# The expert number of a search is formed on GpSimd instead of VectorE, between two gathers

## What is computed

```python
s1, i1 = lax.top_k(s[:, :, 0], PEER_TOPK)            # 16 best of 128 keys, twice
s2, i2 = lax.top_k(s[:, :, 1], PEER_TOPK)
cand_s = (s1[..., :, None] + s2[..., None, :]).reshape(T, PEER_HEADS, PEER_TOPK * PEER_TOPK)
cand_e = (i1[..., :, None] * PEER_KEYS + i2[..., None, :]).reshape(T, PEER_HEADS, PEER_TOPK * PEER_TOPK)
top_s, sel = lax.top_k(cand_s, PEER_TOPK)
eid = jnp.take_along_axis(cand_e, sel, axis=-1)      # the expert numbers
gate = jax.nn.softmax(top_s, axis=-1)
act = jax.nn.gelu(jnp.einsum('thkd,td->thk', u_tab[eid], xt).astype(jnp.float32), approximate=False)
w = (gate * act).astype(xt.dtype)
return jnp.einsum('thk,thkd->td', w, v_tab[eid])
```

## Time and profile before

| | |
|---|---|
| median of 3 runs | 3986.89 us (3982.22 to 3993.07) |
| the profiled execution | 3986.96 us, its span 3984.8 us |
| VectorE busy | 2691.8 us, 68% |
| GpSimd busy | 1225.4 us, 31%, 1024 gathers and 64 casts |
| TensorE busy | 3115.6 us, 78% |
| moved by the DMA engines | 1295.14 MB, of it 1073.81 MB by gathers |

### The profile page before, as it was taken

The page is one execution under the profiler, slowest core; times in us unless marked ns, Lnnn a source line. Parts: engine busy times, 40 slices in busy tenths (PEclk is TensorE's granted clock), DMA queues, the critical chain, the costliest instruction groups (busy, mean ns, idle before and its releaser), DMA issues. The chain is left out here.

```text
span 3984.8 us, 31095 instructions
## 1 busy us (share of the span) xinstructions
PE 3115.6 (78%) x7816; PEld 1412.6 (35%) x7816; DVE 2691.8 (68%) x5254; ACT 1377.4 (35%) x3574; POOL 1225.4 (31%) x1092
## 2 busy tenths in 40 slices
PE   8979999897889989878777877888765656556656
PEld 4545555543434434433333332333322222222222
DVE  3345545312477767777778777868888887888884
ACT  3213333202344344334333423343333334334332
POOL 0000000000233324433344343434444444444442
PEclk9988898798999999989889998889888878878887
DMA  4330101255899999999999999999999999999996
GB/s 160 118 141 24 44 29 37 97 209 222 349 393 414 393 360 421 418 418 378 417 398 417 361 393 391 426 355 411 424 412 399 424 419 389 420 414 393 426 422 265
DMA packets 212916, 1295.14 MB, mean 325 GB/s; under 512 B 24608, under 2 KB 38176, under 8 KB 69408
## 3 DMA queue, kind: packets, MB, share of 16 engines
q0 software_dynamic: 147456, 1073.81, 65.5%
q1 hardware_dynamic: 59552, 207.15, 13.8%
q10 hardware_dynamic: 5760, 12.59, 0.8%
HBM read 1253.60 MB, written 39.85 MB: 325 GB/s over the span
## 5 line engine op out<-in xcount | busy, mean ns | idle before, releaser
L1297 PE MATMUL l_acc<-l_rows,l_diag 128*128 128x512 f32 x2560 | 1422.6, 698 | 732.0 <-ACT l_diag L1431 718.4
L1198 POOL DMA_INDIRECT l_rows<-in_peer_uv,l_at x1024 | 1189.6, 1162 | 1732.1 <-DVE l_acc L1577 1082.3
L1567 DVE SCALAR_TENSOR_TENSOR l_rows<-l_rows,l_xn 128x1024 f32<-128x1024 f32 x1024 | 1227.1, 1224 | 320.2 <-DMA l_rows<-in_peer_uv,l_at 259.8
L1297 PEld LDWEIGHTS l_acc<-l_rows,l_diag 128*128 128x128 f32 x2560 | 526.2, 218 | 1563.6 <-ACT l_diag L1431 1025.8
L1577 DVE SCALAR_TENSOR_TENSOR l_acc<-l_rows,l_wts,l_acc 128x1024 f32<-128x1024 f32 x384 | 492.6, 1283 | 135.0 <-ACT l_wts L1427 135.0
L1423 ACT ACTIVATE l_dots<-l_dots 128x2 f32<-128x2 f32 x512 | 103.8, 203 | 1080.8 <-DVE l_rows L1567 1076.0
L1191 POOL CAST l_at<-l_expert 128x16 uint32<-128x16 f32 x64 | 35.7, 557 | 978.8 <-DVE l_expert L1553 978.5
L117 PE MATMUL l_pa<-all_ring,l_xt 128*128 128x512 f32 x656 | 296.9, 604 | 17.6 <-DMA l_xt<-kept_xnt 17.2
L117 PE MATMUL l_pa<-l_ring,l_xt 128*128 128x512 f32 x624 | 285.1, 608 | 18.2 <-DMA l_xt<-kept_xnt 12.3
L1427 ACT ACTIVATE l_wts<-l_dots,l_gates 128x1 f32<-128x1 f32 x1024 | 293.5, 287 | 16.8
L1431 ACT ACTIVATE l_diag<-all_ident,l_wts 128x128 f32<-128x128 f32 x640 | 257.1, 402 | 21.0
(11 more groups left out here) (241 smaller groups left out, 2780.4 us busy)
## 6 DMA issues: line engine op xcount, KB each, us to landing
l_ring<-in_w_late SPq DMA_DIRECT2D x44, 1024.0 KB
all_ring<-in_w_late SPq DMA_DIRECT2D x44, 1024.0 KB
l_rows<-in_peer_uv,l_at POOLq DMA_INDIRECT x1024
l_yt<-kept_yt SPq DMA_DIRECT2D x48, 256.0 KB, 12.4
kept_s<-l_yt ACTq DMA_DIRECT2D x32, 256.0 KB
l_s_in<-kept_s SPq DMA_DIRECT2D x64, 128.0 KB
mix_w_branches<-in_w_branches_kept SPq DMA_DIRECT2D x8, 768.0 KB, 4.5
kept_yt<-b_yt SPq DMA_DIRECT2D x8, 768.0 KB
```

The costliest lines, as they stand in the source:

```text
L1198: pool.indirect_dma_start(out=rows[:, r % SLOTS, :], out_offset=None, in_=A["peer_uv"], in_offset=bass.IndirectOffsetOnAxis(ap=at[:, c % 2 ...
L1297: ins = pe.matmul(acc2[:, hs], diag[n_pe(r) % DIAGS][:], rows[:, r % SLOTS, D + half * HB:D + (half + 1) * HB], start=first, stop=last)
L1567: dve.scalar_tensor_tensor(out=u, in0=u, scalar=1.0, in1=xn[:, t % 2, :], op0=ALU.mult, op1=ALU.mult, accum_out=dots[:, n:n + 1]).then_inc ...
```

## The change

VectorE keeps only the comparison of `choose`. Product and sum go to GpSimd: one product of 512 elements to a partition, then five additions that each halve the 32 lanes of a winner (256, 128, 64, 32 and 16 elements), then the cast of lane 0, strided, into `at`. GpSimd does this for head c+1 between the 12th and the 13th gather of head c, and for head 0 ahead of the first gather. `hot` isn't doubled, so VectorE's next `search_pairs` waits until the cast is done, and ScalarE's next `convert` waits until the product has read `top_f`.

```diff
+CHOSEN_AT = 12
...
         @block.gpsimd
         def _(pool):
+            hots = [P, TOPK, 2, TOPK]
+
+            def choose(q):
+
+                pool.wait_ge(marked, q + 1)
+                pool.tensor_tensor(hot[:], hot[:], top_f[:].unsqueeze(1).to_broadcast(hots), ALU.mult).then_inc(picked, 1)
+                pool.wait_ge(picked, q + 1)
+                width = 2 * TOPK
+                lanes = hot[:].rearrange("p a k b -> p a (k b)")
+                for n in range(5):
+                    width //= 2
+                    pool.tensor_tensor(lanes[:, :, 0:width], lanes[:, :, 0:width], lanes[:, :, width:2 * width], ALU.add).then_inc(added, 1)
+                    pool.wait_ge(added, q * 5 + n + 1)
+                pool.tensor_copy(at[:, q % 2, :], lanes[:, :, 0]).then_inc(at_ready, 1)
+
             def row(r):
 
                 c, n = divmod(r, TOPK)
+                if c == 0 and n == 0:
+                    choose(0)
+                if n == CHOSEN_AT and c + 1 < PH * T:
+                    choose(c + 1)
                 if n == 0:
-                    pool.wait_ge(chosen, c + 1)
-                    pool.tensor_copy(at[:, c % 2, :], expert[:, c % 3, :]).then_inc(at_ready, 1)
                     pool.wait_ge(at_ready, c + 1)
...
             def convert(q):
 
                 act.wait_ge(parts_ready, q + 1)
+                wait(act, picked, q)
...
             def search_pairs(q):
+                wait(dve, at_ready, q)
...
             def choose(q):
                 dve.wait_ge(converted, q + 1)
-                wait(dve, at_ready, q - 2)
-                order(tt(hot[:], part_f[:].rearrange("p k a -> p a k").unsqueeze(3).to_broadcast(hots),
-                         R["iota16"][:].unsqueeze(1).unsqueeze(1).to_broadcast(hots), ALU.is_equal))
-                order(tt(hot[:], hot[:], top_f[:].unsqueeze(1).to_broadcast(hots), ALU.mult))
-                ins = dve.tensor_reduce(expert[:, q % 3, :], hot[:].rearrange("p a k b -> p a (k b)"), AX.X, ALU.add)
-                ins.then_inc(chosen, 1)
-                dve.wait_ge(chosen, q + 1)
+                tt(hot[:], part_f[:].rearrange("p k a -> p a k").unsqueeze(3).to_broadcast(hots),
+                   R["iota16"][:].unsqueeze(1).unsqueeze(1).to_broadcast(hots), ALU.is_equal).then_inc(marked, 1)
                 dve.wait_ge(exp_ready, q + 1)
```

More of the change, by code:

```diff
@@ L994, in late_stage @@
         soft, total = sb("soft", [P, 2, TOPK]), sb("total", [P, 2, 3])
-        expert, gates = sb("expert", [P, 3, TOPK]), sb("gates", [P, 3, TOPK])
+        gates = sb("gates", [P, 3, TOPK])
         at = sb("at", [P, 2, TOPK], U32)
@@ L1030, in late_stage @@
         (merged_done, rms_done, rms_ready, xs_ready, prms_done, prms_ready, prstd_ready, out_ready, dve_step, act_step,
-         searched, best_ready, parts_ready, converted, neg_ready, exp_ready, sum_ready, gate_ready, chosen, at_ready,
+         searched, best_ready, parts_ready, converted, neg_ready, exp_ready, sum_ready, gate_ready, marked, picked, added, at_ready,
          dot_done, act_done, wts_ready, diag_ready, acc_done, acc2_done, h2_ready, h2t_ready) = (sem(n) for n in (
              "merged_done rms_done rms_ready xs_ready prms_done prms_ready prstd_ready out_ready dve_step act_step "
-             "searched best_ready parts_ready converted neg_ready exp_ready sum_ready gate_ready chosen at_ready "
+             "searched best_ready parts_ready converted neg_ready exp_ready sum_ready gate_ready marked picked added at_ready "
              "dot_done act_done wts_ready diag_ready acc_done acc2_done h2_ready h2t_ready").split())
```

## The result

The changed kernel takes 4060.22 us (median of 4 runs, 4054.83 to 4069.88) against 3986.95: a ratio of 1.0195, 95% interval 1.0175 to 1.0216 (the quotient of the two medians is 1.0184). It is 73 us slower. I had said 4070.

A forecast was written before the change was run, and what follows sets the result against it. No engine was full; DMA transfers limited the second stretch, gathers from 2700 to 3900 us. Late queue 64 + 36, prologue 3, less 17 for VectorE's freed time: +86 us on 3986.96, so 4073, said as 4070; range 3960 to 4180.

The forecast's parts named there:

- The allowance: Between the 12th and 13th gathers: GpSimd may start the next gather 4.1 us late before the DMA engines run dry.
- The block's length: GpSimd's seven instructions ahead of the 13th gather: 3.5 + 1.2 + 1.6 = 6.3 us, between 3.0 and 12.1.
- The price of a late queue: Gathers behind the block: queue dry 2.2 us a head; 64 us for 29 saturated heads, 36 for 33 earlier ones.
- The credit for VectorE's freed time: VectorE loses 1.44 us a head: nothing directly in the saturated stretch, 17 us gained in the first.
- faster: Rival, chance 0.17: slots limit, not the queue; VectorE's freed time brings slots free sooner, around 3950 us.
- New waits: Candidate sum and ScalarE's conversion don't wait for the block; the first gather in the prologue comes 3 us later.
- GpSimd gives way, VectorE doesn't: Rule weighed for SBUF reads: casts wait for dots, dots never lengthen; a product would hold VectorE by the skill's rule.
- Where the waits for rows show: Sign in VectorE's dots: waits up from 3.5 us a head, the largest on the row issued behind the block.
- DMA share: Sign in the stretch from 2700 to 3900 us: share down from 1.00 to about 0.95.
- heavy: Rival, chance 0.12: each GpSimd instruction waits for a whole VectorE instruction; block 12.1 us, about 4350 us.
- my case: Main forecast, chance 0.50: late gathers slow the kernel to between 4010 us (block 4.8 us) and 4180 (block 9 us).

The follow-up runs named there:

- three pauses: The kernel before with 20, 32 or 42 dependent 16-element GpSimd memsets ahead of each head's 13th gather, VectorE's work kept: 1.0033, 1.0143 and 1.0278.
- the run with 32 memsets: The kernel before with 32 dependent 16-element GpSimd memsets ahead of each head's 13th gather, VectorE's work kept: 4035.7 us, ratio 1.0143.

## Why the prediction was right, step by step

- **The allowance (4.1 us).** Right, as far as three pauses can tell: 3.9 us of pause cost 0.33%, 6.0 us 1.43%. They place the bend near 4 us and not to a tenth, and the 13 us for a pause inside the allowance were not in my sum. It came from four gathers in flight, 2.45 us a row and 6.4 us for a gather into an empty queue.
- **The block's length (6.3 us).** Right, 6.1 us in the head shown, and in part by luck. GpSimd's instructions by shape in the first block, with nothing beside them:

```profile
L1192 POOL TENSOR_TENSOR l_hot<-l_hot,l_top_f 128x512 f32<-128x512 f32 x1 | 1.3, 1262 | 973.9 <-DVE l_hot L1569 973.9
L1198 POOL TENSOR_TENSOR l_hot<-l_hot 128x256 f32<-128x256 f32 x1 | 0.7, 726 | 0.1
```

  The slope is (1262 - 726) ns over 256 elements, 2.09 ns, twice VectorE's as I had put it, and the seven take 3.4 us for my 3.5. But the six gaps come to 0.45 us where I had 1.2, and the waits against VectorE in the head shown to 2.05 us where I had 1.6 (5.91 us from the product's start to the cast's end, for 3.86 in the first block). The two errors offset each other for the most part.
- **The price of a late queue.** Right in direction, too high in size. I charged 2.2 us a head in the second stretch and half of that in the first, 64 + 36 us. By GB/s the whole loss is 48 + 27, and the pause of the block's length costs only 1.43%, some 56 us. The error is that I let each microsecond beyond the allowance cost a whole one in the second stretch and a half in the first. The pauses show 0.7 to 0.8 in the second stretch, and 0.33 to 0.5 over all heads.
- **The credit for VectorE's freed time (17 us).** Wrong: worth nothing (1.0007). This also settles the *faster* rival: less work on VectorE brings no slot free soon enough to matter. That the number came so close, 86 predicted for 73, is partly luck: the queue was charged 100 us where a pause of that length costs 56, the credit was 17 us too high, and the 16 to 20 us (0.4 to 0.5%) that the changed kernel loses on top of such a pause stood nowhere in the sum.
- **New waits.** Right. VectorE's candidate sum and ScalarE's conversion don't wait for GpSimd: neither stands in the view of waits with GpSimd as the one waited for. The first gather starts 4.15 us after the product's start where it was 1.95: 2.2 us, I had 3.
- **GpSimd gives way, VectorE doesn't.** I left open what a product would do. It holds VectorE: 2802 ns for a dot. The Trainium skill (SBUF — State Buffer, "Who interferes with whom") says that a VectorE instruction with two SBUF inputs and a GpSimd instruction that reads SBUF exclude each other. The trace now agrees on both sides: the dot of 2802 ns, and a cast of 16 elements that takes 1.07 us at 3533.76 beside a dot. The holding also spoils a number of mine: VectorE's busy time fell by 33 us and not by 88, because 55 us of holding are counted in it.
- **Where the waits for rows show.** I expected the largest at the row behind the block. They come three rows later and in the next head. The 13th row has several microseconds between landing and its dot: by the landings in the trace, 3.8 us in the mean of heads 34 to 62, for 4.0 before, because its transfer, issued late, takes 5.1 us from the issue's end for 8.8 before.
- **DMA share.** I expected 0.95 and it is 0.98; the rate tells it better, 397 for 413 GB/s.
- The *heavy* rival's mechanism exists (the block ahead of the 9th gather, 9.25 us in one head), but not in the place that the change chose.
- The bounds of my case don't follow from their own terms: 3987 + 223 - 14 is 4196, where I wrote 4180, and a block of 4.8 us gives 4005 for 4010. The measured time lies far from both.

**What is left.** The changed kernel's 1.0195 stands 0.4 to 0.5% above the pauses of its length (1.0143 and 1.0152, the interval of the second overlaps with it). The rates say it too, in both stretches: 389 and 397 GB/s, for 391 and 400 in the run with 32 memsets and 391 and 399 in the run without product and sum and with 30 memsets. The granted clock doesn't explain it, 0.887 in the changed kernel's profiled execution and 0.888 in that last run's. That reads cost something just where the queue is thin would fit: the held weighing frees a slot later. No run isolates it, so it stays open. No placement made the kernel faster than before. The run without product and sum (1.0007, 0.9994 to 1.0019) leaves none to gain more than 0.06% by VectorE's freed time.

## What to carry to other kernels

Here the engine that issues the transfers had an allowance between two issues: what is in flight, times the time of one transfer, less the latency into an empty queue, 4.1 us. Work put there was almost free up to it (0.33%). Beyond it, each microsecond cost 0.7 to 0.8 us where the transfers run back to back, and 0.33 to 0.5 us over the whole kernel. Work out the same three numbers for your kernel. Cut the work up and put the pieces where the issuer waits for a slot anyway: four pieces apart cost 0.17%, three close together 1%. And before moving work off an engine, ask what its time is worth: in this kernel, nothing.

## What the hardware showed that I hadn't expected

- GpSimd's product of 512 elements holds a VectorE instruction with two inputs: dots of 1224 ns reached 2802 ns, weighings of 1281 ns 2703 ns. Beside casts of 16 elements alone, in the kernel before, no dot lasted over 1295 ns and no weighing over 1341.
- A chain of seven dependent GpSimd instructions beside back-to-back dots and weighings is stretched from 4.15 to 9.25 us in one head with the block ahead of the 9th gather, in which VectorE starts six of them. In that run's mean from 3100 to 3500 us the five additions took 0.7 to 1.4 us each, by their sizes, where alone they take 0.2 to 0.7. Ahead of the 13th gather, where VectorE searches between its dots, it stays at 6.
- A memset of 16 elements and the wait for it take 0.167 us (3.33 us for 20), where I had taken 0.3.
